# One page group weighted in every step, maxima ahead of pages, exponentials ahead of copies

## Time and profile before

| | |
|---|---|
| median of 3 runs | 1157.97 us (1156.71 to 1161.84) |
| the profiled execution | 1155.58 us, of which the profile's span is 1153.9 us |
| mean granted TensorE clock | 0.964 of full speed |
| busy | PE 1045.1 us, VectorE 609.7 us, ScalarE 378.0 us, POOL 170.6 us |
| transfers | 170.93 MB, mean 148 GB/s |

### The profile page before, as it was taken

The page is one execution under the profiler, slowest core; times in us unless marked ns, Lnnn a source line. Parts: engine busy times, 40 slices in busy tenths (PEclk is TensorE's granted clock), DMA queues, the critical chain, the costliest instruction groups (busy, mean ns, idle before and its releaser), DMA issues.

```text
span 1153.9 us, 26835 instructions
## 1 busy us (share of the span) xinstructions
PE 1045.1 (91%) x10642; PEld 964.7 (84%) x10642; DVE 609.7 (53%) x1253; ACT 378.0 (33%) x774; POOL 170.6 (15%) x257
## 2 busy tenths in 40 slices
PE   3899999999999999998899989678777789999995
PEld 2899999999999999997799977555545549999995
DVE  4366454451688821495765355767668542332432
ACT  6321112212233222154542222444545412332433
POOL 3002310000320000103504500123333100000000
PEclk9899999999999999999899989798999889999998
DMA  9446743223344443237456845567787786223213
GB/s 281 102 139 115 167 118 94 71 69 93 114 119 129 115 131 92 73 93 226 124 158 183 257 167 161 157 214 242 251 251 255 235 203 215 74 80 102 73 37 148
DMA packets 202059, 170.93 MB, mean 148 GB/s; under 512 B 37755, under 2 KB 166246, under 8 KB 200134
## 3 DMA queue, kind: packets, MB, share of 16 engines
q1 hardware_dynamic: 179078, 120.75, 37.5%
q0 software_dynamic: 11392, 28.52, 8.0%
q10 hardware_dynamic: 11496, 20.36, 4.8%
HBM read 141.93 MB, written 25.31 MB: 145 GB/s over the span
## 4 chain that ended last, share of the span: by engine, by line
PE 72%; DMA 9%; DVE 6%; issue 5%; ACT 4%; SPq 3%; POOLq 0%; ACTq 0%; POOL 0%; DVEq 0%
PE gemm L2065 12%; PE gemm L2066 12%; PE gemm L2067 12%; PE gemm L2420 5%; PE gemm L2422 5%; PE gemm L2421 5%; DMA kpe<-cache_kpe 4%; PE misc L2141 2%; PE misc L2336 2%; PE misc L2151 1%; PE misc L2092 1%; DMA w_raw<-w_glu 1%; DMA w_raw<-w_in 1%; PE gemm L2350 1%; DMA osr<-u_d 1%
## 5 line engine op out<-in xcount | busy, mean ns | idle before, releaser
L2065 PE MATMUL gemm<-xh,w_hi 128*128 128x260 f32 (+2 forms) x1056 | 302.3, 286 | 0.3 <-DVE w_lo L1333 0.3
L2066 PE MATMUL gemm<-xl,w_hi 128*128 128x260 f32 (+2 forms) x1056 | 300.7, 285 | 0.0
L2067 PE MATMUL gemm<-xh,w_lo 128*128 128x260 f32 (+2 forms) x1056 | 299.9, 284 | 0.0
L1333 DVE TENSOR_TENSOR w_lo<-w_raw,w_hi 128x2048 fp32r<-128x2048 f32 (+3 forms) x63 | 109.6, 1739 | 225.3 <-ACT w_hi L857 221.7
L857 ACT ACTIVATE w_hi<-w_raw 128x2048 fp32r<-128x2048 f32 (+3 forms) x63 | 90.7, 1439 | 337.2 <-PE gemm L2067 281.7
L2065 PEld LDWEIGHTS gemm<-xh,w_hi 128*128 128x128 f32 x1056 | 198.8, 188 | 1.2 <-DVE w_lo L1333 0.5
L2067 PEld LDWEIGHTS gemm<-xh,w_lo 128*128 128x128 f32 x1056 | 199.1, 189 | 0.0
L2066 PEld LDWEIGHTS gemm<-xl,w_hi 128*128 128x128 f32 x1056 | 198.9, 188 | 0.0
L2420 PE MATMUL gemm<-comb_hi,w_hi 128*128 128x260 f32 x512 | 147.7, 289 | 1.2 <-DVE comb_lo L1945 1.1
L2421 PE MATMUL gemm<-comb_lo,w_hi 128*128 128x260 f32 x512 | 145.3, 284 | 0.0
L2422 PE MATMUL gemm<-comb_hi,w_lo 128*128 128x260 f32 x512 | 145.3, 284 | 0.0
(11 more groups left out here) (383 smaller groups left out, 1990.2 us busy)
## 6 DMA issues: line engine op xcount, KB each, us to landing
w_raw<-w_in SPq DMA_DIRECT2D x35, 1024.0 KB, 6.3
ckv<-cache_ckv POOLq DMA_DIRECT2D x74, 256.0 KB, 4.3
w_raw<-w_out SPq DMA_DIRECT2D x16, 1024.0 KB, 5.8
ckv<-cache_ckv SPq DMA_DIRECT2D x54, 256.0 KB, 4.3
z_d<-ev ACTq DMA_DIRECT2D x16, 260.0 KB, 2.0
w_raw<-w_glu SPq DMA_DIRECT2D x8, 512.0 KB, 4.3
yt<-x_prompt SPq DMA_DIRECT2D x4, 1024.0 KB
o_y_p<-yt SPq DMA_DIRECT2D x4, 1024.0 KB
```

The source lines that it names most:

```text
L1333: dve.tensor_tensor(w_lo[:, slot, 0:width], w_raw[:, slot, 0:width], w_hi[:, slot, 0:width].bitcast(F32), ALU.subtract).then_inc(w_lo_read ...
L2065: pe.matmul(acc, a, xa, start=k == 0, stop=False)
L2066: pe.matmul(acc, a, xb, start=False, stop=False)
L2067: last = pe.matmul(acc, b, xa, start=False, stop=k == k_tiles - 1)
```

## The change

Five edits belong together. `freed_at` gives every step one group: group i is weighted in step i + 4, and sample 6's four in steps 28 and 29; in steps that do not begin a head PE weights it ahead of `turn_weights`. VectorE takes `maximum(n+1)` ahead of the first half of the pages, waits ahead of each half for the one queue that brings it, and does `normalise(n+1)` between the halves. ScalarE does `exponential(n+1)` ahead of `copy_turned(n)` in all steps. `osr` is cut into two tiles that no longer lie over the sample weights. POOL zeroes both as soon as the last page scores are made, and SP loads them ahead of `wuv`.

```diff
-        osr = at("osr", A0 + 50688, [P, N_SAMPLE - 2, KV_LORA])
+        osr = [at("osr0", A0 + 50688, [P, 3, KV_LORA]), at("osr1", A0 + 59456, [P, 3, KV_LORA])]
...
         def freed_at(i):
-            return 4 * (i // 4) + 4 + (2 if i % 4 >= 2 and i // 4 < N_SAMPLE - 2 else 0)
+            return i + 4 if i // 4 < N_SAMPLE - 2 else 4 * (N_SAMPLE - 1) + i % 4 // 2
...
             sp.wait_ge(sc_ready, N_PAIRS)
+            sp.wait_ge(rows_stored, 64 * (N_SAMPLE - 2))
+            for part in range(2):
+                sp.wait_ge(filled, 12 + part)
+                for j in range(4):
+                    sp.dma_start(osr[part][32 * j:32 * j + N_HEADS],
+                                 u_d.rearrange("(b p) t -> p b t", p=P)[32 * j:32 * j + N_HEADS, 3 * part:3 * part + 3, 0:KV_LORA]
+                                 ).then_inc(sample_loaded, 16)
             sp.wait_ge(weights_ready, N_SAMPLE)
             sp.dma_start(wuv[:], w_uv).then_inc(wuv_loaded, 16)
-            sp.wait_ge(filled, 12)
-            sp.wait_ge(rows_stored, 64 * (N_SAMPLE - 2))
-            for j in range(4):
-                sp.dma_start(osr[32 * j:32 * j + N_HEADS], u_d.rearrange("(b p) t -> p b t", p=P)[32 * j:32 * j + N_HEADS, 0:N_SAMPLE - 2, 0:KV_LORA]
-                             ).then_inc(sample_loaded, 16)
...
             pool.wait_ge(sc_ready, N_PAIRS)
-            pool.wait_ge(weights_ready, N_SAMPLE)
-            pool.memset(osr[:], 0.0).then_inc(filled, 1)
+            for part in range(2):
+                pool.memset(osr[part][:], 0.0).then_inc(filled, 1)
...
-                if n % 4 == 0:
+                if n + 1 < N_TILES:
                     exponential(n + 1)
-                    if n:
-                        sample_weights(n // 4 - 1)
-                    if n and n // 4 + 1 < N_HEADS:
+                if n % 4 == 0 and n:
+                    sample_weights(n // 4 - 1)
+                    if n // 4 + 1 < N_HEADS:
                         head_hi(n // 4 + 1)
                 copy_turned(n)
-                if n % 4 and n + 1 < N_TILES:
-                    exponential(n + 1)
...
             def turn_pages(n, first, last):
-                if first == 0:
-                    for by_sync, count in enumerate(loaded_counts(n)):
-                        if count:
-                            dve.wait_ge(page_loaded[by_sync][n % RING], count)
-                    if n >= 3:
-                        dve.wait_ge(sc_ready, (n - 3) // 2 + 1)
+                by_sync = (1 if first == 0 else 0) if n >= RING else (1 if n == BY_SYNC else 0)
+                dve.wait_ge(page_loaded[by_sync][n % RING], loaded_counts(n)[by_sync])
+                if first == 0 and n >= 3:
+                    dve.wait_ge(sc_ready, (n - 3) // 2 + 1)
...
                 if n + 1 < N_TILES:
+                    maximum(n + 1)
                     turn_pages(n + 1, 0, 2)
                 if n % 4 == 0 and n:
                     turn_sample_weights(n // 4 - 1)
                 if n + 1 < N_TILES:
-                    maximum(n + 1)
+                    normalise(n + 1)
                     turn_pages(n + 1, 2, 4)
                     turn_rotary(n + 1)
                 if n % 4 == 0 and n:
                     gate_o(n // 4 - 1)
-                if n + 1 < N_TILES:
-                    normalise(n + 1)
...
-                turn_weights(n)
+                    turn_weights(n)
                 for i in range(N_GROUPS_OF_PAGES - 4):
                     if freed_at(i) == n:
                         weigh_pages(i // 4, i % 4)
+                if n % 4 or not n:
+                    turn_weights(n)
```

More of the change, by code:

```diff
@@ L2436, in _ @@
             pe.wait_ge(o_copied, 8)
-            pe.wait_ge(sample_loaded, 16 * 9 + 64)
+            pe.wait_ge(sample_loaded, 16 * 9 + 128)
             for q in range(2):
                 for j in range(4):
-                    pe.matmul(T_BANK[q][32 * j:32 * j + N_HEADS, :], wcomb[:, 4 * q + j, :], (osr[:, 4 * q + j, :] if 4 * q + j < N_SAMPLE - 2 else osb[:, j % 2, :]), start=True, stop=False)
+                    pe.matmul(T_BANK[q][32 * j:32 * j + N_HEADS, :], wcomb[:, 4 * q + j, :], (osr[(4 * q + j) // 3][:, (4 * q + j) % 3, :] if 4 * q + j < N_SAMPLE - 2 else osb[:, j % 2, :]), start=True, stop=False)
                 for j in range(4):
```

## The result

The median went from 1158.86 us (20 runs) to 1152.98 us (20 runs): ratio 0.9946, 95% interval 0.9931 to 0.9961, 5.9 us off. The forecast had 14 off, with the loop a part of the gain. The profiled execution took 1153.92 us (span 1152.2).

A forecast was written before the change was run, and what follows sets the result against it. It took the loop from freed place to landed page to freed place to set the attention loop's pace. Front 2.0, loop 2.0, loop's end 1.0 and tail 9.2 made 14.2 us off: 1144 us median, range 1128 to 1157.

The forecast's parts named there:

- the loop: Page loop over five operand-loading heads: 24.95 us per head against 25.36, 2.0 us off, with 10.5 off and 10 more as ends.
- The front: Steps before the first weights: maxima and exponentials run earlier, 2.0 us off (0 to 2.04).
- a head's three terms: Head's first issue to late half's transpose 15.9 us, to sample maximum's end 4.6, next sample group's transpose to next issue 4.45.
- the landing: Second group's half on SP, from its last issue to its transpose: 6.7 us taken, added to 9.2 us of issues.
- the rule set against the rows: Skill's DMA rule: a page takes 2.6 us, half there 11.8 us after first issue, time near 1120 us; chance 0.03.
- SP's queue becomes the bound: Rival: second group's half waits behind a head's operands on SP, each us later costs one per head; above 1160 us; chance 0.12.
- the gain is the tail's wait alone: Rival: loop gives back some 4 us, front gains nothing; 1157 us, 1152 with the clock kept; range 1152 to 1158, chance 0.22.
- spread transfers land sooner: Rival: one group per step flattens bursts, heads 23.25 us, at most down to 22; 1135.5 us, range 1126 to 1138, chance 0.23.
- The end of the loop: Last group: the maximum runs during VectorE's page wait; 1.0 us off (0 to 2).
- The tail: After the loop: early `osr` saves 4.2 us of wait, full clock 3.5 in the combination and 1.5 in eighteen products; 9.2 off.
- the clock falls anyway: Case for the products after the loop: PE's clock drops despite early `osr`, leaving 4.2 us off of 9.2; no separate chance.

The follow-up runs named there:

- two groups at a time: Changed kernel with the old `freed_at` (two groups in a sample's first step, two in its third); ratio 0.9897 to the kernel before.
- half ahead: Changed kernel with SP asking for the second group's half ahead of a later head's queries and keys; ratio 0.9855 to the kernel before.
- the kernel before with operands later: Kernel before with only a later head's queries and keys asked for behind the third and fourth groups' halves; ratio 0.9932.
- the operands later: Changed kernel with pages ahead of a later head's queries and keys, these one step later, behind the third group's half; 1130.40 us, ratio 0.9715.
- the run alone: Kernel before with only the edits behind the loop (`osr` in two tiles, zeroed and loaded early, ahead of `wuv`); ratio 0.9939, 7.1 us off.

## Why the prediction was wrong

**The front: right.** Forecast 2.0 off. From the first `turn_weights` to the first sample maximum, four kernels with VectorE's old order took 22.25 to 24.51 us (mean 23.1), and nine with the new one 19.40 to 21.98 (mean 21.0): 2.1 off.

**The loop: wrong, and in sign.** Forecast 2.0 off for five heads, measured 4.6 on. Of a head's three terms, the last two were right: from the transpose that waits to SP's next first issue 9.05 us were forecast, 9.1 measured (8.3 to 8.8 in four heads, 11.6 in the third, where PE stopped for 2.48 us as told in the last section). The issues ahead of the half were right: 9.2 us forecast, 9.0 in the mean of the five heads. The step that failed is the landing: "I take 6.7, near the second group's value, because it stands behind the same kinds of transfers". It took 5.6 to 9.8 us, mean 8.1, so the half was there 17.1 us after the head's first issue in place of 15.9. The reason given was wrong on both counts. The second half before has no queries and keys ahead of it, and there was not less to move: at the last issue of that half some 2.1 MB had been asked for on all queues and had not landed, the half included, against 1.2 MB before (means of five heads, worked out from the traces' issues and landings). From the last issue of an SP half to its last landing, means of the five heads:

| the half, and the kernel | right behind the operands | not behind them |
|---|---|---|
| second group, before / after | 8.1 (after) | 5.7 (before) |
| second group, two groups at a time / half ahead | | 5.7 / 5.5 |
| third group, before / the half ahead | 8.0 / 7.4 | |
| third group, the kernel before with operands later | | 4.1 |

So the nearest row was the third group's, not the second's: what counts is not the group but what was asked for just ahead, here queries and keys. The prediction had both numbers (9.1 and 7.3 to the transpose), and the head that gave its 7.3 had the longest landing of the five (7.2 us; the others 4.9 to 5.9). With 9.1, the third group's value, its own sum gives heads of 9.2 + 9.1 + 9.05 = 27.35 us, the end it had worked out; with the table's 8.0, 26.25, where 26.28 was measured. "Each us that it lands later costs one us per head" holds only up to the next late half: moved forward, the second landed 4.8 us earlier (12.3 after the head's first issue), and a head gained only 2.5.

The Trainium skill, DMA: Bandwidth & Descriptors, section Queues, rings and completion order, says that each DMA engine consumes the descriptors of one queue in ring order. The table fits that, but does not show that SP's own queue is the whole cause. POOL's half of the second group, with no operands in its queue, took 7.1 us from its last issue to its landing in the changed kernel and 5.3 with the half ahead. And with the operands later the fourth group's half stands right behind them and took 5.9 us, not 8. So the load of all queues takes part; no run separates the two.

The 2.6 us of the rule set against the rows did not come: SP's halves in these heads of the changed kernel took 3.2 to 9.8 us. The section of the Trainium skill cited there (DMA: Bandwidth & Descriptors, Anatomy of one DMA) is on transfers that GpSimd issues, and these are SP's.

The rival "SP's queue becomes the bound" had the mechanism right. Against it stood that "nothing in the trace took that long", which was true of the 10.7 us at which it would have been slower than before, and no reason to take 6.7.

The rival "the gain is the tail's wait alone" came nearest in its numbers: the half landing at 7.9 us, 4 us given back by the loop and, with the clock kept, 1152 us. Measured were 8.1 us, 4.6 us and 1152.98 us. In part that is luck: it had no gain in the front, which gave 2.1.

**What went unpriced.** The groups behind do gain, as forecast (step 8 waits no more). But the end of the burst did not move: the fourth group's half landed 21.7 us after the head's first issue, and 22.6 before. The DMA engines still run at 0.97 for 20 us and then at 0.07:

```profile
755.00:775.00 20.00, 13.80 (x354) 9.73 (x353) 12.01 (x22) 8.64 (x30) 8.58 (x16) 0.92 0.97 303
775.00:780.50 5.50, 5.47 (x48) 2.81 (x51) 5.26 (x17) 1.70 (x6) 0.00 (x0) 0.69 0.07 21
```

The rival "spread transfers land sooner" needed another edit: the operands out of the way. With it heads of 22.55 us were reached, near the 22 us that the rival gave as its foot.

**The end of the loop: right.** From SP's first issue of the last head to the last sample maximum 19.48 us, before 20.14: 0.7 off, forecast 1.0.

**The tail: right, its last term not.** 7.5 off by the profile and 7.1 by the run alone, forecast 9.2. The wait and the way to it gave 4.3 (19.02 us from the last sample maximum, then 14.69; forecast 4.2); the combination 3.25 (7.16 us, then 3.91; forecast 3.5); the eighteen products nothing (3.72, then 3.78; forecast 1.5), since the clock was at 0.54 there again. That part of the rival "the clock falls anyway" came true in this execution, for those products alone. It is not so in every profile: in seven of the ten kernels with the new end they took 2.3 us at 1.00, as forecast, but in five of these the clock had been lower earlier (0.90 from the last sample maximum to the combination), and that way took 16.4 us in place of 14.7. `wuv` behind the small issues cost nothing that shows.

**The sum.** 2.1 off, 4.1 on (174.0 us in two kernels with the old loop, 178.1 in two with the new one, end of the loop included) and 7.5 off make 5.5 off; measured were 5.9. The time lay inside the range, and the chance for faster was rightly the largest, but for the tail and the front; of the 14 us forecast, 5.9 came. Of the 8 us missing the heads are 6.6 (2.0 off forecast, 4.6 on measured), nearly all of it the landing. The loop's sign was carried by the choice of one row.

**A version that beats both.** The changed kernel with the pages ahead of a later head's queries and keys, and these one step later, takes 1130.40 us, 0.9715 of the kernel before: one moved block of SP's issues, added to the change, is worth four times what the change gave. It is not worth that alone. In the kernel before, the move gave 0.7% (0.9932), the edits behind the loop gave 0.6% (0.9939) and the loop's edits nothing (1.0026); added up that is an estimate of 0.990. The loop's edits pay only once the operands are out of the way.

## What to carry to other kernels

When a transfer is moved in its issuer's order, price it by the row of a transfer that already stands behind the same neighbours, and by the mean over all heads, not by the sibling with the same name in one head. List what a queue carries by when it is needed: loads for a later head go behind the pages that this step waits for, and try that order together with a new schedule of the engines that compute: here it decided whether the schedule was worth anything. When one late transfer is cured, expect only the distance to the next late one, and look again at what its wait had hidden.

## What the runs showed of the hardware that was not expected

PE stops in the middle of its own work, waiting for nothing that the profile names:

```profile
793.78 0.60 PE L2347 MATMUL gemm<-ct,qx 128*32 128x64 f32 x28
797.83 0.22 PE L2347 MATMUL gemm<-ct,qx 128*32 128x64 f32 x1 [3.44 <-issue]
```

The trace has packets of 16 KB on an instruction queue (65 in the whole run). One ended at 796.44, 1.39 us ahead of this restart. The changed kernel has five such stops of 1.4 to 3.4 us in its page scores, each with such a packet ending 1.26 to 1.63 us ahead of its end; in the run with two groups at a time one lasted 5.0 us (790.86 to 795.86, packet to 794.48). That they are waits for code is read from this agreement; no run here varied it. Of the 25 such packets that ended between 720 and 927 us in the changed kernel, eight were followed within 1.9 us by the end of a stop of over 0.3 us that has no named cause, 13.4 us in all; in the kernel before it was five of 26 and 8.3 us. The Trainium skill, Runtime: NRT & Kernel Launch, section Instruction fetch mechanics, calls the crossing of such a block mostly hidden; that is so for the other 17, and these eight showed.

Some of the loop's loss may lie in these stops; no run separates them. They do not explain the order of the kernels: with the half ahead they come to 13.2 us, and that kernel is faster.
